# Second attention: the third chunk's transposes inside the next slab, and one output taken ahead of the third exponentials

## The chip, the cores and the metric

One core of one Trainium2 chip runs the kernel in one launch. The metric is device time in microseconds (us), the median of several runs; lower is better. TensorE (PE in the profile) multiplies and transposes, VectorE (DVE) and ScalarE (ACT) do the elementwise work and read PSUM, SyncE (SP) queues the weight loads, GpSimd (POOL) queues three loads and does nothing else.

## The reference

Two transformer-like blocks over 512 tokens of width 1024, in fp32. The change touches the second block's attention alone, a banded attention with 16 query heads, 4 key and value heads, blocks of 128 queries and a band of three key blocks:

```python
scores = jnp.einsum("bnqkgd,bnskd->bnkgqs", qb, kb)
scores = jnp.where(valid[None, :, None, None], scores + alibi, NEG_INF_2)
m = jnp.maximum(jnp.max(scores, axis=-1, keepdims=True), sink_l)
p = jnp.exp(scores - m)
denom = jnp.sum(p, axis=-1, keepdims=True) + jnp.exp(sink_l - m)
o = jnp.einsum("bnkgqs,bnskd->bnqkgd", p / denom, vb)
```

Beside it the same block computes `u` and `g_lru`, two projections of the normalised input; `u` goes through a depthwise convolution over four tokens, `g_lru` through a gelu.

## The kernel before, in words

**Slabs.** All weights stream through the chip as slabs of 512 KB (`load`, line 390). ScalarE rounds each slab to a high part (`split`, line 427), VectorE subtracts to get the low part (`split`, line 823), and TensorE multiplies in three terms: high by high, high by low, low by high. `gemm` (line 1411) does one slab: in the second attention 8 tiles of three matmuls each, 24 matmuls of 128x512, into one PSUM bank. Its argument `then` maps a tile's number to something that TensorE does right after that tile. A slab waits for its low part, and for the bank to be read out.

**Units.** The second attention (`Attention` object `att2`) has 16 units: 4 query blocks, and for each 4 groups of four heads. The first and the last query block have two key chunks in their band, the middle ones three, so units 0 to 3 and 12 to 15 have two chunks and units 4 to 11 three. For one unit the chain is: TensorE computes scores (line 1571), VectorE makes logits (line 1066), their maximum (line 1073) and three tiny operations (1074 to 1077), ScalarE takes exponentials (lines 580 and 583), TensorE transposes them chunk by chunk (line 1602, four transposes for a chunk), ScalarE copies each transposed chunk to SBUF (line 607), TensorE spreads the inverse sums (line 1582) and multiplies by the values (line 1612), ScalarE copies that out (`take_outputs`, line 589) and VectorE scales it (`outputs`, line 1088).

**Slabs between units.** Each unit is paired with one slab of other work, so that TensorE has something to do: slab 0 stands after scores 0, and slab u + 1 between unit u's transposes and its product with the values. Even slabs give `u`, odd slabs the gelu input. The `u2` and `g2` slabs all go to one PSUM bank (`PLACE`, bank 0 of `gp`), so slab k + 1 can't start until ScalarE has read slab k out. For an even slab that is one copy (`inputs2` on ScalarE, line 697, by way of `take`, line 486, its ACTIVATE on line 489), after which VectorE runs the convolution (lines 1299 to 1304). For an odd slab ScalarE first rounds the convolution's result (line 704) and then takes the gelu (also line 489), which needs another function table than the exponentials do. VectorE takes the low part of the convolution's result (`a_low`, line 855).

**The order of each engine** is written out by hand and each engine works strictly through it.

- ScalarE, for each u (`attention`, line 569): take outputs of u - 1; copy the transposed chunks of u; split a slab; exponentials of u + 2; `gate(u + 1)`, which reads out slab u + 1.
- VectorE, for each u (`attention`, line 1052): inverse sums of u + 1; outputs of u - 1; logits of u + 2; then `between(u + 1)`: split a slab, then the convolution or the low part.
- TensorE, for each u (`attention`, line 1562): transposes of chunks 0 and 1; scores of u + 2; the transposes of chunk 2, where there is one; slab u + 1; inverse sums spread; product with the values.

**Waits that matter here.** The transposed chunks alternate between two banks, so a chunk's transposes wait for ScalarE's copy of the chunk two before it (`pt_ready`): chunk 2 waits for the copy of chunk 0. The exponentials alternate between two buffers (`A.logit[u % 2]`), so VectorE's logits of u + 2 overwrite what unit u's transposes read, and wait until all of them are done:

```python
                    if u >= 2:
                        dve.wait_ge(pt_done, A.done[u - 2])
```

The first attention (`att1`) uses the same code with two chunks at most.

Of the kernel before, what the change touches and what calls it, by code (L numbers as in the profile page):

```python
# [68 lines left out]
STAGE = [("zb", 0)]  # L69
# [3 lines left out]
SLAB, _n = {}, 0  # L73
# [24 lines left out]
MIX_SLAB = {key: SLAB["mix"] + i for i, key in enumerate(STAGE)}  # L98
MIX_GATES = [key for key in STAGE if key[0] != "lru"]
# [22 lines left out]
def build(nc, slabs, params, s5p, s5bt, s5b, s5c, bias1, nd2, x_in, out):  # L122

    ctx = ExitStack()
    with ctx:
# [3 lines left out]
        def sem(name):  # L129
            return ctx.enter_context(nc.semaphore(name))  # L130
# [129 lines left out]
        nb_ready, ex_done = sem("maximum_ready"), sem("exponentials_done")  # L260
# [95 lines left out]
        att1 = Attention(0, 0, 1, 1, 0, Q, KV, 0, 1, VT1, logit1, PT1, "sinks", "y1")  # L356
        att2 = Attention(len(att1.units), att1.done[-1], 2, 1, 1, Q2, KV2, 0, 2, VT2, logit2, PT2, "sinks2", "")

        def by_heads(v):
            return v.rearrange("p (h q) -> p h q", h=2)  # L360
# [63 lines left out]
        def _(act):  # L424
            S = Tally(act, act_step)

            def split(n):

                if n >= NSLAB:
                    return  # L430
                act.wait_ge(s_raw[n % RAW], 16 * (n // RAW + 1))
                if n >= RING:
                    act.wait_ge(half_done, 2 * (n - RING + 1))
                nc.scalar.activation(w_hi[:, n % RING, :], raw[:, n % RAW, :], ACT.Copy).then_inc(w_hi_ready, 1)  # L434
# [110 lines left out]
            n = 0  # L545
# [23 lines left out]
            def attention(A, slab0, gate):  # L569

                for pp in range(A.pairs):
                    act.wait_ge(vt_done, pp + 1 + (A.u0 > 0))
                    nc.scalar.activation(A.vt[:, pp, :, :].rearrange("p a b -> p (a b)"), mp[:, 3 + pp, :],
                                         ACT.Copy).then_inc(vt_ready, 1)

                def exponentials(u):
                    row = mini[u % 3]
                    lo, hi = A.span(u)
                    act.wait_ge(nb_ready, A.u0 + u + 1)
                    nc.scalar.activation(row[:, 3, :], row[:, 2, :], ACT.Exp)  # L580
                    for h in range(4):
                        L = A.logit[u % 2][:, h, lo:hi]
                        ins = nc.scalar.activation(L, L, ACT.Exp, bias=row[:, 1, h:h + 1], scale=1.0 / A.units_of_logit,  # L583
                                                   accum_out=row[:, 4, h:h + 1])
                    ins.then_inc(ex_done, 1)

                def take_outputs(u):
                    act.wait_ge(at_done, A.u0 + u + 1)
                    nc.scalar.activation(A.of_heads(A.q, u), by_heads(mp[:, 5, 0:2 * P]), ACT.Copy).then_inc(at_copied, 1)

                def outputs_hi(u):
                    act.wait_ge(at_read, A.u0 + u + 1)
                    nc.scalar.activation(A.of_heads(h_hi, u), A.of_heads(A.q, u), ACT.Copy).then_inc(h_hi_ready, 1)

                n = len(A.units)
                split(slab0 + AHEAD)
                exponentials(0)
                gate(0)
                exponentials(1)
                if A.name:  # L600
                    z_chunk(CT - 1)
                for u in range(n):
                    if u:
                        take_outputs(u - 1)
                    for g, j, _ in A.chunks[u]:
                        act.wait_ge(pt_done, g + 1)
                        nc.scalar.activation(A.pt[:, j, :], mp[:, 3 + g % 2, :], ACT.Copy).then_inc(pt_ready, 1)
                    if A.name and u:
                        outputs_hi(u - 1)
                    if u + 1 < n:  # L610
                        split(slab0 + u + 1 + AHEAD)
                    if u + 2 < n:
                        exponentials(u + 2)
                    if u + 1 < n:
                        gate(u + 1)
                take_outputs(n - 1)
                if A.name:
                    outputs_hi(n - 1)

            def gate_s(u):  # L620
                take("gate_s", u, gate2[u], func=ACT.Tanh, scale=0.5)

            attention(att1, SLAB["gate_s"], gate_s)


# [784 lines left out]
        def _(pe):  # L1410
# [52 lines left out]
            def a_stage(name, k, ready=None, then={}):  # L1463
                gemm(name, k, 8, 1, a, al, ready, then=then)
# [97 lines left out]
            def attention(A, between):  # L1562
                def scores(u):
                    b, pp, _ = A.units[u]
                    lo, hi = A.span(u)
                    k_lo, k_hi = A.keys(u)
                    for i, p, h4, _ in A.lanes(u):
                        rows = slice(HD * p, HD * p + HD)
                        if A.u0 + u:
                            pe.wait_ge(lane_read, 4 * (A.u0 + u - 1) + i + 1)  # L1570
                        pe.matmul(A.scores(i)[:, lo:hi], A.q[rows, 4 * pp + h4, b * P:(b + 1) * P],  # L1571
                                  A.kt[rows, A.k0 + pp, k_lo:k_hi], start=True, stop=True).then_inc(sc_done, 1)

                def spread_inverse(u):

                    pe.wait_ge(inv_ready, A.u0 + u + 1)
                    if A.u0 + u:
                        pe.wait_ge(at_read, A.u0 + u)
                    for h in range(2):
                        for p in range(2):  # L1580
                            lane = mini[u % 3][:, 5, 2 * p + h:2 * p + h + 1]
                            pe.matmul(mp[HD * p:HD * p + HD, 5, (2 + h) * P:(3 + h) * P], lane.to_broadcast([P, HD]), ident,
                                      start=True, stop=True, skip_group_check=True)

                n = len(A.units)
                scores(0)
                between(0)
                scores(1)
                if A.name:
                    outputs(CT - 1)  # L1590
                    pe.wait_ge(z_val, CT)
                pe.wait_ge(vt_ready, A.pairs + (A.u0 > 0))
                for u in range(n):
                    b, pp, _ = A.units[u]
                    pe.wait_ge(ex_done, A.u0 + u + 1)
                    for x, (g, j, kb) in enumerate(A.chunks[u]):
                        if x == 2 and u + 2 < n:
                            scores(u + 2)
                        if g >= 2:
                            pe.wait_ge(pt_ready, g - 1)  # L1600
                        for h in range(4):
                            ins = pe.transpose(mp[:, 3 + g % 2, h * P:(h + 1) * P],  # L1602
                                               A.logit[u % 2][:, h, j * P:(j + 1) * P], ident)
                        ins.then_inc(pt_done, 1)
                    if u + 2 < n and len(A.chunks[u]) < 3:
                        scores(u + 2)
                    between(u + 1)
                    spread_inverse(u)
                    for x, (g, j, kb) in enumerate(A.chunks[u]):
                        pe.wait_ge(pt_ready, g + 1)  # L1610
                        for p in range(2):
                            ins = pe.matmul(mp[HD * p:HD * p + HD, 5, 0:2 * P], A.vt[:, pp, kb, HD * p:HD * p + HD],  # L1612
                                            A.pt[:, j, 2 * P * p:2 * P * (p + 1)], start=x == 0,
                                            stop=x == len(A.chunks[u]) - 1, skip_group_check=True)
                    ins.then_inc(at_done, 1)
# [16 lines left out]
            pe.wait_ge(v_read, CT)  # L1632
            pe.wait_ge(out_read, OUT["gate_a"] + 7)
            transpose_values(att1)
            attention(att1, lambda u: a_stage("gate_s", u) if u < len(att1.units) else None)
            pe.wait_ge(h_lo_ready, H_AT["y1"] + len(att1.units))
            for j in range(COUNT["branch_a"]):
                gemm("branch_a", j, 4, 2, h, hl)
# [32 lines left out]
                    a_stage(name, k)  # L1671
            pe.wait_ge(out_read, OUT["v2"] + 2)
            transpose_values(att2)
            def mix_slab(key):
                gemm("mix", MIX_SLAB[key] - SLAB["mix"], 8, 1, h, hl, first=MIX_GATES.index(key))

            def inputs2(u):
                if u == 0:
                    pe.wait_ge(h_lo_ready, H_AT["xn"] + DC)
                if u < len(att2.units):  # L1680
                    gemm("u2", u, 8, 1, h, hl)
                else:
                    pe.wait_ge(lane_read, 4 * (att2.u0 + len(att2.units)))
                    mix_slab(STAGE[0])

            attention(att2, inputs2)

# [194 lines left out]
```

## Time and profile before

| | |
|---|---|
| Median of 3 runs | 1509.76 us (1509.2 to 1511.92) |
| The profiled execution's own time | 1511.41 us |
| Its span in the profile | 1509.6 us |
| TensorE busy | 1432.3 us, 95% |
| VectorE busy | 867.6 us, 57% |
| ScalarE busy | 619.9 us, 41% |
| The second attention | about 786 to 959 us of the span |
| Granted TensorE clock over the span, mean | 0.981 |

The time is a little more than the span, since it includes what lies around the recorded instructions. Times inside the profile count from the span's start. A busy share says how much of the span an engine worked, not whether anybody waited for it: for that the chain of waits and the timelines have to be read.

### The profile page before, as it was taken

What the parts mean: (1) busy time and instruction counts of PE and PEld (TensorE: products, weight loads), DVE (VectorE), ACT (ScalarE), POOL (GpSimd) and SP (SyncE); (2) the same over time, 40 slices, a digit from 0 to 9 for tenths busy, and PEclk for the clock granted to TensorE, in tenths of its full rate; (3) what the DMA queues carried; (4) which work ended last, traced back from release to release, by engine and by line L of the source; (5) the groups of instructions that cost most, each with busy time, mean ns of one, the idle gap of its engine ahead of it and who ended that gap; (6) DMA issues with size and microseconds to landing.
All of it is one profiled execution on the core that took longest, in us unless ns stands there. A gap on an engine that the chain in (4) does not pass through costs nothing.

```text
span 1509.6 us, 17696 instructions
## 1 busy us (share of the span) xinstructions
PE 1432.3 (95%) x7240; PEld 1153.6 (76%) x7240; DVE 867.6 (57%) x1227; ACT 619.9 (41%) x986; POOL 1.9 (0%) x7
## 2 busy tenths in 40 slices
PE   6999999998999999998998999989799999999997
PEld 5877677777788888887776667767588888888885
DVE  7887644646636364455567766488754443443445
ACT  5452653333313222233245677778543221232232
POOL 0000000000000000000000000000000000000000
PEclk9999999999999999998999999999999999999998
DMA  4222123231323323233131111222232232333323
GB/s 160 88 81 89 54 70 126 86 110 34 112 88 95 111 84 111 85 98 98 44 97 56 43 56 57 77 69 78 84 98 73 96 109 87 98 98 99 97 88 108
DMA packets 36560, 131.62 MB, mean 87 GB/s; under 512 B 4432, under 2 KB 4560, under 8 KB 36224
## 3 DMA queue, kind: packets, MB, share of 16 engines
q1 hardware_dynamic: 36128, 127.16, 26.9%
q0 software_dynamic: 352, 3.34, 0.6%
q8 instruction: 57, 0.93, 0.3%
q14 instruction: 23, 0.19, 0.0%
HBM read 128.39 MB, written 2.10 MB: 86 GB/s over the span
## 4 chain that ended last, share of the span: by engine, by line
PE 74%; DVE 15%; ACT 8%; issue 2%; DMA 1%; SPq 0%; DVEq 0%; ACTq 0%
PE gp L1426 21%; PE gp L1427 21%; PE gp L1428 21%; DVE w_lo L828 2%; ACT arena L583 2%; DVE arena L1066 1%; DVE arena L1073 1%; ACT w_hi L434 1%; PE mp L1602 1%; ACT a_hi L458 1%; PE mp L1571 1%; PE mp L1452 1%; PE mp L1612 1%; PE mp L1426 1%; PE mp L1427 1%
## 5 line engine op out<-in xcount | busy, mean ns | idle before, releaser
L1426 PE MATMUL gp<-h_hi,w_hi 128*128 128x512 f32 x944 | 374.5, 397 | 24.9 <-ACT arena L719 13.5
L1427 PE MATMUL gp<-h_lo,w_hi 128*128 128x512 f32 x944 | 371.0, 393 | 0.0
L1428 PE MATMUL gp<-h_hi,w_lo 128*128 128x512 f32 x944 | 370.7, 393 | 0.0
L828 DVE TENSOR_TENSOR w_lo<-raw,w_hi 128x1024 fp32r<-128x1024 f32 x232 | 283.2, 1222 | 147.9 <-ACT w_hi L434 146.9
L434 ACT ACTIVATE w_hi<-raw 128x1024 fp32r<-128x1024 f32 x232 | 243.1, 1051 | 165.8 <-DMA raw<-slabs 92.9
L1426 PE MATMUL gp<-a_hi,w_hi 128*128 128x512 f32 x704 | 276.3, 393 | 1.2 <-DVE w_lo L828 1.1
L1428 PE MATMUL gp<-a_hi,w_lo 128*128 128x512 f32 x704 | 274.1, 389 | 0.0
L1427 PE MATMUL gp<-a_lo,w_hi 128*128 128x512 f32 x704 | 274.0, 389 | 0.0
L1426 PEld LDWEIGHTS gp<-h_hi,w_hi 128*128 128x128 f32 x944 | 179.5, 190 | 68.8 <-issue 24.7
L1428 PEld LDWEIGHTS gp<-h_hi,w_lo 128*128 128x128 f32 x944 | 179.4, 190 | 38.2
L1427 PEld LDWEIGHTS gp<-h_lo,w_hi 128*128 128x128 f32 x944 | 179.8, 190 | 36.5
L1426 PEld LDWEIGHTS gp<-a_hi,w_hi 128*128 128x128 f32 x704 | 132.1, 188 | 32.3 <-issue 3.3
L1428 PEld LDWEIGHTS gp<-a_hi,w_lo 128*128 128x128 f32 x704 | 132.2, 188 | 27.9
L1427 PEld LDWEIGHTS gp<-a_lo,w_hi 128*128 128x128 f32 x704 | 132.2, 188 | 26.6
L668 ACT ACTIVATE h_hi<-arena 128x512 fp32r<-128x512 f32 x32 | 20.2, 632 | 133.4 <-DVE arena L1205 133.4
L1388 DVE TENSOR_TENSOR arena<-gp,R 128x512 f32<-128x512 f32 x44 | 30.4, 692 | 69.0 <-PE gp L1428 68.9
L804 ACT ACTIVATE a_hi<-arena 128x512 fp32r<-128x512 f32 x22 | 13.9, 633 | 99.5 <-DVE arena L1391 99.5
L1230 DVE TENSOR_TENSOR arena<-arena,gp 128x512 f32<-128x512 f32 x24 | 16.5, 687 | 64.5 <-PE gp L1428 64.5
L489 ACT ACTIVATE arena<-gp 128x512 f32<-128x512 f32 x41 | 24.4, 596 | 63.7 <-PE gp L1428 62.4
L583 ACT ACTIVATE arena<-arena 128x256 f32<-128x256 f32 (+2 forms) x96 | 49.8, 520 | 0.0
L1397 DVE TENSOR_TENSOR arena<-arena,gp 128x512 f32<-128x512 f32 x24 | 16.5, 686 | 57.9 <-PE gp L1428 57.9
L801 ACT ACTIVATE arena<-arena 128x512 f32<-128x512 f32 x22 | 13.9, 632 | 83.5 <-DVE arena L1388 83.5
(248 smaller groups left out, 1505.5 us busy)
## 6 DMA issues: line engine op xcount, KB each, us to landing
raw<-slabs SPq DMA_DIRECT2D x232, 512.0 KB, 3.5
arena<-x_in SPq DMA_DIRECT2D x4, 512.0 KB, 5.8
arena<-x_in POOLq DMA_DIRECT2D x1, 2048.0 KB, 8.7
out_t<-arena SPq DMA_DIRECT2D x8, 256.0 KB, 2.2
arena<-bias POOLq DMA_DIRECT2D x1, 1024.0 KB, 5.2
arena<-s5b SPq DMA_DIRECT2D x1, 512.0 KB, 9.2
arena<-s5c SPq DMA_DIRECT2D x1, 512.0 KB, 10.0
par<-params SPq DMA_DIRECT2D x1, 232.0 KB, 2.6
```

The source lines that it names most:

```text
L434: nc.scalar.activation(w_hi[:, n % RING, :], raw[:, n % RAW, :], ACT.Copy).then_inc(w_hi_ready, 1)
L458: nc.scalar.activation(a_hi[:, c, :], X[:, c, :], ACT.Copy, scale=col(gain, c)).then_inc(a_hi_ready, 1)
L489: nc.scalar.activation(dst, bank(name, m) if src is None else src, func, scale=scale).then_inc(out_read, 1)
L583: ins = nc.scalar.activation(L, L, ACT.Exp, bias=row[:, 1, h:h + 1], scale=1.0 / A.units_of_logit, accum_out=row[:, 4, h:h + 1])
L668: nc.scalar.activation(h_hi[:, k, :], fbuf[k % 2], ACT.Copy).then_inc(h_hi_ready, 1)
L828: TT(w_lo[:, n % RING, :], raw[:, n % RAW, :], w_hi[:, n % RING, :].bitcast(F32), ALU.subtract).then_inc(w_lo_ready, 1)
L1230: TT(Fo[:, m, :], Fo[:, m, :], src, ALU.add).then_inc(out_read, 1)
L1388: TT(tmp[e], take("ff2", s0 + 2 * c + e), R[:, :], ALU.mult).then_inc(out_read, 1)
L1397: TT(X[:, m, :], X[:, m, :], src, ALU.add).then_inc(out_read, 1)
L1426: pe.matmul(dst, hi, x_hi(t), start=t == 0, stop=False)
L1427: pe.matmul(dst, hi, x_lo(t), start=False, stop=False)
L1428: ins = pe.matmul(dst, lo, x_hi(t), start=False, stop=t == tiles - 1)
```

## The change

Two edits, both in the second attention alone. (1) On TensorE the transposes of a unit's third chunk are no longer issued ahead of slab u + 1 but inside it, right behind its tile number 2, that is after nine of its 24 matmuls; scores of u + 2 stand directly in front of the slab, as for units with two chunks. (2) On ScalarE, in the first iteration (u = 0), `gate(1)`, which rounds the first convolution's result and takes the gelu of slab 1, stands ahead of the third exponentials (those of unit 2), not behind them. For all other u the order is as it was. Nothing is added to or taken from what is computed or loaded.

```diff
@@ ScalarE, attention
                     if u + 1 < n:
                         split(slab0 + u + 1 + AHEAD)
+                    if u == 0 and not A.name:
+                        gate(1)
                     if u + 2 < n:
                         exponentials(u + 2)
-                    if u + 1 < n:
+                    if u + 1 < n and (u or A.name):
                         gate(u + 1)
@@ TensorE, attention
                     b, pp, _ = A.units[u]
-                    pe.wait_ge(ex_done, A.u0 + u + 1)
-                    for x, (g, j, kb) in enumerate(A.chunks[u]):
-                        if x == 2 and u + 2 < n:
-                            scores(u + 2)
+                    def turn_chunk(g, j, u=u):
                         if g >= 2:
                             pe.wait_ge(pt_ready, g - 1)
                         for h in range(4):
                             ins = pe.transpose(mp[:, 3 + g % 2, h * P:(h + 1) * P],
                                                A.logit[u % 2][:, h, j * P:(j + 1) * P], ident)
                         ins.then_inc(pt_done, 1)
-                    if u + 2 < n and len(A.chunks[u]) < 3:
+
+                    pe.wait_ge(ex_done, A.u0 + u + 1)
+                    for g, j, _ in A.chunks[u][:2]:
+                        turn_chunk(g, j)
+                    if u + 2 < n:
                         scores(u + 2)
-                    between(u + 1)
+                    third = A.chunks[u][2:]
+                    between(u + 1, {2: lambda: turn_chunk(*third[0][:2])} if third else {})
                     spread_inverse(u)
@@ TensorE, inputs2 and mix_slab
-                    gemm("u2", u, 8, 1, h, hl)
+                    gemm("u2", u, 8, 1, h, hl, then=then)
                 else:
                     pe.wait_ge(lane_read, 4 * (att2.u0 + len(att2.units)))
-                    mix_slab(STAGE[0])
+                    mix_slab(STAGE[0], then)
```

`between` for the first attention takes the new argument and leaves it unused.

## Rows read from the trace of the kernel before

**Rows 1.** Stretches: length, busy of PE, PEld, DVE, ACT, POOL, granted clock, DMA.

```profile
808.00:830.00 22.00, 20.69 (x106) 15.28 (x108) 14.19 (x31) 13.76 (x32) 0.00 (x0) 0.85 0.17 57
...
852.00:874.00 22.00, 21.00 (x128) 15.14 (x128) 15.29 (x29) 15.31 (x35) 0.00 (x0) 1.00 0.15 49
```

**Rows 2.** Who waited for whom, 786 to 960 us: total, times, longest.

```profile
DVE arena L1066 <- PE mp L1602: 3.1, 4, 0.8
PE mp L1602 <- ACT arena L607: 3.0, 3, 1.4
```

**Rows 3.** Chain that ended last, 842 to 865 us: start us, us, what.

```profile
842.69 1.87 DVE arena L1066 x4
...
849.56 0.52 ACT a_hi L704
...
851.40 0.60 ACT arena L489
...
864.48 1.87 DVE arena L1066 x4
```

**Rows 4.** TensorE's timeline: start us, us, line, operation, count, idle before and its releaser.

```profile
804.91 0.38 PE L1571 MATMUL gp<-arena 64*128 64x256 f32 x1
809.31 0.77 PE L1426 MATMUL gp<-h_hi,w_hi 128*128 128x512 f32 x1 [4.03 <-ACT arena L489]
...
814.14 0.63 PE L1428 MATMUL gp<-h_hi,w_lo 128*128 128x512 f32 x1
...
821.50 0.50 PE L1426 MATMUL gp<-h_hi,w_hi 128*128 128x512 f32 x1
...
823.68 0.39 PE L1426 MATMUL gp<-h_hi,w_hi 128*128 128x512 f32 x1
...
831.22 0.47 PE L1426 MATMUL gp<-h_hi,w_hi 128*128 128x512 f32 x1
```

**Rows 5.** ScalarE's timeline, 804 to 818 us, same columns.

```profile
804.57 0.20 ACT L580 ACTIVATE arena<-arena 128x4 f32<-128x4 f32 x1 [3.59 <-DVE arena L1077]
...
807.28 1.28 ACT L489 ACT_TABLE_LOAD   x1
808.57 0.60 ACT L489 ACTIVATE arena<-gp 128x512 f32<-128x512 f32 x1
...
813.11 0.21 ACT L580 ACTIVATE arena<-arena 128x4 f32<-128x4 f32 x1 [0.45 <-DVE arena L1077]
...
817.65 0.60 ACT L489 ACTIVATE arena<-gp 128x512 f32<-128x512 f32 x1 [2.36 <-PE gp L1428]
```

**Rows 6.** VectorE's timeline, 800 to 822 us, same columns.

```profile
800.32 0.75 DVE L1304 SCALAR_TENSOR_TENSOR arena<-arena,par 128x511 f32<-128x511 f32 x1
...
818.28 0.55 DVE L1299 TENSOR_SCALAR arena<-arena,par 128x512 f32<-128x512 f32 x1 [4.07 <-ACT arena L489]
...
821.69 1.48 DVE L1066 SCALAR_TENSOR_TENSOR arena<-arena,mp 128x384 f32<-128x384 f32 x3
```

**Rows 7.** TensorE's timeline round a third chunk's transposes, 840 to 853 us.

```profile
840.84 0.66 PE L1602 MATMUL mp<-par,arena 128*128 128x128 f32 x4
...
850.88 0.48 PE L1571 MATMUL gp<-arena 64*128 64x384 f32 x1
852.81 0.66 PE L1602 MATMUL mp<-par,arena 128*128 128x128 f32 x4 [1.44 <-ACT arena L607]
```

**Rows 8.** Timelines of ScalarE (the gelu of slab 13) and TensorE (slab 14's start).

```profile
934.23 0.60 ACT L489 ACTIVATE arena<-gp 128x512 f32<-128x512 f32 x1
...
935.95 0.50 PE L1426 MATMUL gp<-h_hi,w_hi 128*128 128x512 f32 x1
```

**Rows 9.** TensorE's timeline after two waits elsewhere.

```profile
396.01 0.47 PE L1426 MATMUL gp<-h_hi,w_hi 128*128 128x512 f32 x1 [2.40 <-issue]
...
1037.23 0.77 PE L1426 MATMUL gp<-h_hi,w_hi 128*128 128x512 f32 x1 [2.83 <-ACT arena L719]
...
1039.93 0.47 PE L1426 MATMUL gp<-h_hi,w_hi 128*128 128x512 f32 x1
```

More of the change, by code:

```diff
@@ L1634, in _ @@
             transpose_values(att1)
-            attention(att1, lambda u: a_stage("gate_s", u) if u < len(att1.units) else None)
+            attention(att1, lambda u, then={}: a_stage("gate_s", u) if u < len(att1.units) else None)
             pe.wait_ge(h_lo_ready, H_AT["y1"] + len(att1.units))
@@ L1673, in _, with mix_slab, inputs2 @@
             transpose_values(att2)
-            def mix_slab(key):
-                gemm("mix", MIX_SLAB[key] - SLAB["mix"], 8, 1, h, hl, first=MIX_GATES.index(key))
-            def inputs2(u):
+            def mix_slab(key, then={}):
+                gemm("mix", MIX_SLAB[key] - SLAB["mix"], 8, 1, h, hl, first=MIX_GATES.index(key), then=then)
+            def inputs2(u, then={}):
                 if u == 0:
```

## The prediction

> **What bounds the kernel now.** I read the page's busy shares first (TensorE 95%), then the busy time by stretch: in the second attention TensorE is busy 20.69 to 21.00 of 22 us, VectorE and ScalarE some 14 to 15, and the clock is below full in one stretch alone [rows 1]. That looks like a stage bound by TensorE. The waits say otherwise: TensorE's third-chunk transposes stood for ScalarE's copy three times, 3.0 us in all, and VectorE's logits stood for those transposes four times, 3.1 us in all [rows 2]. So VectorE and ScalarE wait in a ring, and the chain of waits runs through them, not through TensorE.
>
> The ring in the part with three chunks, from the chain: logits of unit 6 start at 842.69, ScalarE reaches the rounding for the gelu at 849.56 and the gelu at 851.40, done 852.00; TensorE's third-chunk transposes follow at 852.81 and are done at 853.47; logits of 7 come right behind, and logits of 8 start at 864.48 [rows 3, 7]. One turn is two units and takes 864.48 - 842.69 = 21.79 us. What TensorE needs for one such unit without waiting is read between the third-chunk transposes of unit 4 (840.84) and the end of the next scores (850.88 + 0.48 = 851.36): 10.52 us, so 21.04 for two [rows 7]. TensorE has 0.75 us to spare in each turn. Nobody waits for it but VectorE, at the third-chunk transposes.
>
> Earlier there is one large hole: scores of unit 3 end at 804.91 + 0.38 = 805.29, and slab 2 starts at 809.31, after 4.03 us, since its bank is freed by the gelu of slab 1. Behind the hole the clock is at the lower level (1.2 GHz): matmuls come every 0.43 us until about 814.6, where 13 have gone by; at the upper level (2.4 GHz) nine take 823.68 - 821.50 = 2.18 us, with the start of a slab in it [rows 4, 5].
>
> **Edit 2, the gelu ahead of the third exponentials.** The gelu of slab 1 needs the first convolution (done at 800.32 + 0.75 = 801.07 [rows 6]) and slab 1, which ends some 0.6 us later. ScalarE is free at 801.0. New order: rounding 0.52 [rows 3], one table load (1.29 from start to next start [rows 5]), gelu at about 803.0, done 803.6 (0.60 [rows 5]). TensorE comes to slab 2 at 805.29, so the 4.03 us are gone, and with them the slow stretch: 13 matmuls of 0.43 against about 0.24, 2.5 us. On TensorE alone that is 6.5 us.
>
> The ring gets less. The exponentials' table goes in from 803.5 to 804.8, so those of unit 2 start at 804.84 in place of 804.57 [rows 5] and end at 807.0. Inverse sums and outputs on VectorE take it to 807.7. Logits of a unit with two chunks take 3.3 us to the exponentials (3.50 from the convolution's end at 801.07 to 804.57, with 0.2 of inverse sums in it [rows 5, 6]). So exponentials of unit 3 start at 810.9 or 811.0, not at 813.11, and need no table load: the loads are as many as before, two, and both now stand ahead of unit 2. They end at 813.1. Slab 2 (24 matmuls, 5.8 us) ended at 811.1, so its copy comes at 813.1, not 817.65, and is done at 813.7; the convolution starts then, not at 818.28 [rows 5, 6]. Everything up to the logits of unit 4 (821.69 before) moves with it: **4.6 us gained**. It is kept as long as the ring is the bound.
>
> A rule of the Trainium skill speaks against this edit: "ScalarE: Activation LUTs", section What ACT_TABLE_LOAD costs, gives every switch of table set some 1.28 us of load and 1.38 us of drain behind it. The trace agrees with the load (1.28 [rows 5]) and not with a drain: the gelu starts 1.29 us after its load did. By the page's figures both switches ahead of unit 2's exponentials would cost 2.8 us more, the gain would be 1.8, and the sum below 2.8 us higher.
>
> **Edit 1, the transposes inside the slab.** Their four waits don't go away: the buffer that VectorE's logits overwrite is still free only when the third chunk is turned. Before, in units 5, 7, 9 and 11, they came 0.81 us behind the gelu (852.00 to 852.81). Now the slab comes first. It can't start before the gelu frees the bank, at 852.00 in the same count; then nine matmuls take 2.18 us, and the change from slab to transposes about 0.1 (my estimate, from 0.32 against 0.23 at a slab's start). The transposes start 2.28 us behind the gelu, the logits 1.47 us later than before. Four times: **5.9 us lost**, all on the ring.
>
> Unit 4 is the first with three chunks. Its transposes were early enough before (840.84 + 0.66 = 841.50, logits at 842.69). Now slab 4 starts behind the gelu of slab 3, 4.6 us earlier than 831.22 at 826.6; slab 5 follows after 840.84 - 831.22 = 9.62 at 836.2; the transposes are done at 836.2 + 2.28 + 0.66 = 839.2, while VectorE is ready at 842.69 - 4.6 = 838.1. **1.1 us lost**. In units 6, 8 and 10 the convolution (3 us on VectorE) covers them, by 0.2 us only: slab 6 at 848.5, slab 7 at 859.2, transposes done 862.1, VectorE ready 862.4. If that cover fails, some tenths each are added.
>
> **At the end** part of the delay is absorbed. Slab 14 started at 935.95 when TensorE got there, 1.12 us after the gelu of slab 13 was done (934.23 + 0.60 = 934.83); from there on TensorE is never waiting long [rows 8]. A ring that is later by 5.9 + 1.1 - 4.6 = 2.4 us moves slab 14 by 2.4 - 1.1 = **1.3 us**. What stands behind the second attention starts from its end and moves with it. Taking TensorE out of a slab and back costs it about 0.2 us in eight units, 1.6 us, hidden in its waits. VectorE's and ScalarE's splits are covered: ScalarE's behind the third copy has still over a microsecond before the exponentials. SyncE's loads follow VectorE's splits, and are two slabs ahead. The first attention has two chunks at most: nothing.
>
> **The clock.** TensorE now needs 21.2 us of a turn of 21.79 + 1.47 = 23.3, and the 2 us between come in one piece, ahead of slabs 6, 8 and 10 (and 1.9 ahead of slab 4: it gets there at 815.0 + 9.7 = 824.7, the gelu at 826.6). A wait of 1.44 us kept the clock [rows 7], so did one of 2.40 behind slab matmuls [rows 9]; one of 2.83 and one of 4.03 lost it [rows 4, 9]. The new ones lie between, and stand behind transposes and scores. Prices: the short slow stretch, six matmuls in 2.70 us against 1.45, costs 1.25 [rows 9]; at most nine slow matmuls stand ahead of the transposes, 9 x 0.2 = 1.8. I take one loss at 1.5; the bounds are none and four of 1.8.
>
> **Sum.** 1.3 + 1.5 = +2.8 us. It is made against the profiled execution (span 1509.6, own time 1511.41, so 1.8 around it). That execution lies 1.65 above the median of 1509.76; I add the difference to the median: 1512.5.
>
> **Rivals.**
> - *The clock falls at three or four of the new waits.* For: they recur with each turn, behind narrow work. Against: 2.40 held. Price 1.3 + 3.5 x 1.5 to 1.3 + 4 x 1.8, so +6.5 to +8.5: 1516.3 to 1518.3. It decides from the second loss on: two give +4.3, beyond 3.0 us, which is 0.2% and about what a measurement of this kernel can tell from no change. Slower. Two or more: 0.33.
> - *TensorE is the bound after all.* For: 95% busy. Then the change gives the hole and slow stretch (6.5), and the 3.0 us of waits ahead of slabs [rows 2], less 1.6 for the broken slabs: -7.9, 1501.9. Against: the ring's 21.79 against 21.04. Weaker form: VectorE's wait costs less than worked, and part of the 4.6 is kept, -3 to 0. Together 0.17.
> - *Table switches cost more in the new place*: +5.6, 1515.4. Against: the row. 0.03.
> - *It doesn't do what it says*: if slab 1 or the convolution came late, ScalarE would stand at the gelu with the exponentials behind it. Both are there within 1 us of need; 0.03, about +1 to +3.
>
> **Numbers.** Forecast (none or one loss of the clock, errors of some tenths in the terms) 0.44, own range 1510.3 to 1514.0. For 8 in 10 the range reaches up to four losses at 1.6 (+7.7) and down to half of the 4.6 us kept (-2.3): 1507.5 to 1517.5. Slower by over 0.2%: 0.33 and 0.03 from the rivals of the clock and the tables, 0.05 from the upper end of the forecast's own range, 0.41. Faster by over 0.2%: 0.11 of TensorE's 0.17. Within: the rest, 0.48.
>
> **What would show it.** Right: slab 2 starts near 805.3 with no wait; the convolution of slab 2 near 813.7; in the chain a turn of about 23.2 in place of 21.8; VectorE's waits for line 1602 at 2.2 us, not 0.8; TensorE's waits ahead of slabs 4, 6, 8, 10 for line 489, 1.7 to 2 us each, and none for line 607; the mix stage about 1 to 3 us later. Wrong: logits of 7, 9, 11 directly behind VectorE's own work, or a turn of 21.8 or less; then the price of edit 1 falls away. Slow matmuls (0.43 apart) behind several of the new waits would be the first rival.

## The result, and the profile after

Over 22 runs of each on one chip the kernel after takes 1514.28 us (1511.63 to 1517.67), the kernel before 1511.97 (1509.01 to 1514.63). The ratio of the times is 1.0018, with an interval of 1.0011 to 1.0024: the change costs about 2.7 us (0.0018 x 1511.97). The interval excludes that nothing changed, and the value lies just under the 0.2% that I called no change. 22 runs put before 2.2 us above the 1509.76 of its first three, so differences are read below, not absolute times. The profiled execution after has a span of 1512.3 us and an own time of 1514.08, against 1509.6 and 1511.41 before.

The busy time of the kernel after by stretch in the second attention (columns: stretch, its length, then busy time with number of instructions of TensorE, its weight loads, VectorE, ScalarE and GpSimd; last the clock, the DMA share and GB/s):

```profile
808.00:830.00 22.00, 19.85 (x116) 14.24 (x115) 16.67 (x34) 14.57 (x33) 0.00 (x0) 1.00 0.18 58
852.00:874.00 22.00, 19.95 (x121) 14.15 (x120) 14.79 (x29) 14.44 (x33) 0.00 (x0) 0.99 0.16 49
```

Against [rows 1], the first stretch is at full clock now (0.85 before), and TensorE is busy a microsecond less in the second: it waits more. Where, the waits say (786 to 962 us; who waited for whom, total us, times, longest):

```profile
ACT arena L607 <- PE mp L1601: 17.4, 10, 3.3
...
DVE arena L1068 <- PE mp L1601: 10.9, 6, 3.2
PE gp L1428 <- ACT arena L489: 9.9, 7, 2.1
```

VectorE's logits (line 1068, 1066 before) stood 3.1 us for the transposes [rows 2] and stand 10.9 now. (The edits move line numbers: the transposes, 1602 before, are 1601 after, 1599 in experiment 2 and 1604 in experiment 9; a slab's matmuls, 1426 to 1428 before, are 1428 to 1430.) The longest of these waits is ahead of the logits of unit 9, behind the transposes of unit 7:

```profile
875.70 1.48 DVE L1068 SCALAR_TENSOR_TENSOR arena<-arena,mp 128x384 f32<-128x384 f32 x3 [3.20 <-PE mp L1601]
```

TensorE's waits for ScalarE's third copy are gone from the list, and its waits ahead of slabs for the gelu (line 489) are 9.9 us. The chain of waits, 800 to 880 us:

```profile
803.12 0.60 ACT arena L489
...
813.31 0.49 ACT arena L489
813.83 0.56 DVE arena L1301
...
817.32 1.87 DVE arena L1068 x4
...
839.20 1.96 DVE arena L1068 x4
...
847.99 0.61 ACT arena L489
848.74 0.47 PE gp L1428
...
851.03 0.45 PE mp L1601 x4
851.50 1.96 DVE arena L1068 x4
...
862.47 1.87 DVE arena L1068 x4
```

The gelu of slab 1 is done at 803.72, the convolution of slab 2 starts at 813.83, the logits of unit 4 at 817.32 (818.28 and 821.69 before [rows 6]): 4.4 us gained. Then the slab and the transposes stand in the chain between the gelu and the logits of unit 7, and the turn from unit 6 to unit 8 takes 862.47 - 839.20 = 23.27 us, not the 21.79 of [rows 3]. TensorE's timeline (start, length, engine, line, operation; in brackets the idle time before it and who ended it):

```profile
805.28 0.50 PE L1428 MATMUL gp<-h_hi,w_hi 128*128 128x512 f32 x1
...
826.77 0.47 PE L1428 MATMUL gp<-h_hi,w_hi 128*128 128x512 f32 x1 [2.15 <-ACT arena L489]
...
848.74 0.47 PE L1428 MATMUL gp<-h_hi,w_hi 128*128 128x512 f32 x1 [1.72 <-ACT arena L489]
850.87 0.60 PE L1601 MATMUL mp<-par,arena 128*128 128x128 f32 x4
...
871.92 0.47 PE L1428 MATMUL gp<-h_hi,w_hi 128*128 128x512 f32 x1 [2.05 <-ACT arena L489]
...
874.18 0.63 PE L1430 MATMUL gp<-h_hi,w_lo 128*128 128x512 f32 x1
874.61 1.05 PE L1601 MATMUL mp<-par,arena 128*128 128x128 f32 x4
876.31 0.63 PE L1430 MATMUL gp<-h_hi,w_lo 128*128 128x512 f32 x1
...
938.30 0.47 PE L1428 MATMUL gp<-h_hi,w_hi 128*128 128x512 f32 x1 [0.87 <-ACT arena L489]
```

Slab 2 starts without a wait. The waits ahead of slabs 4, 6 and 8 are 2.15, 1.72 and 2.05 us, slab 10's is 1.73. In the second attention the lower clock (0.63 us a matmul in place of 0.39 to 0.40) comes once, in slab 8. There the transposes start 874.61 - 871.92 = 2.69 us behind the slab's start (2.13 in slab 6) and take some 0.45 longer: 1.0 us. That is the 3.20 in place of the 2.2 us of VectorE's other waits at odd units. The turn that holds it, by VectorE's timeline from 862.39 to 886.85, takes 24.46 us, 1.27 more than the 23.19 of the turn before it. Slab 14 starts 2.35 us later than in [rows 8].

ScalarE's timeline shows the two table loads, the second right behind the gelu:

```profile
801.82 1.28 ACT L489 ACT_TABLE_LOAD   x1
803.12 0.60 ACT L489 ACTIVATE arena<-gp 128x512 f32<-128x512 f32 x1
803.73 1.28 ACT L580 ACT_TABLE_LOAD   x1
805.03 0.20 ACT L580 ACTIVATE arena<-arena 128x4 f32<-128x4 f32 x1
```

Gelu and exponentials start 1.30 us after their loads began.

### The profile page after: what moved, and what is told of

It reads as the page before. It is cut to its first block, busy times and chain, and to the rows that moved or that the text cites. A ratio compares the mean times of both kernels' runs of the same rounds, so it can differ in the third digit from the quotient of the medians.

```text
span 1512.3 us, 17696 instructions
## 1 busy us (share of the span) xinstructions
PE 1433.1 (95%) x7240; PEld 1153.9 (76%) x7240; DVE 867.4 (57%) x1227; ACT 618.5 (41%) x986; POOL 1.9 (0%) x7
## 4 chain that ended last, share of the span: by engine, by line
PE 72%; DVE 15%; ACT 9%; issue 2%; DMA 1%; SPq 0%; DVEq 0%; ACTq 0%
PE gp L1428 21%; PE gp L1429 20%; PE gp L1430 20%; DVE w_lo L830 2%; ACT arena L583 2%; ACT w_hi L434 1%; DVE arena L1068 1%; DVE arena L1075 1%; PE mp L1601 1%; PE mp L1573 1%; DMA raw<-slabs 1%; ACT a_hi L458 1%; PE mp L1454 1%; PE mp L1616 1%; PE mp L1428 1%
```

## The experiments

My theory: edit 2 (the gelu first) gives 4.6 us, edit 1 (the transposes inside the slab) costs more than that, since VectorE and ScalarE, not TensorE, set the turn. The rivals: TensorE is the bound; or it is the break of the slab itself that costs. Each kernel was timed against the kernel before on the same chip; the table stands at the end of this section. A useful measure within one profile is the length of the stage, from the first transposes of values to the first matmul behind the attention: 175.00 us before (785.09 to 960.09), 177.27 after (785.15 to 962.42). It is of use because the start of the stage lies anywhere from 785.09 to 787.30 us in the twelve profiles, behind work that no edit touches, so whole profiled executions differ by up to 2.2 us that have nothing to do with the change.

**1. Edit 2 alone.** Only the change in ScalarE's order; the transposes stay in front.

> Edit 2 alone: ScalarE takes slab 1's gelu ahead of the third exponentials, the third chunk's transposes stay in front of the slab. Theory R (the ring of VectorE and ScalarE sets the pace): 4.5 us faster than the kernel before (3.5 to 5.5), slab 2 near 805.3, logits of unit 4 near 817.3, a turn of 21.7 to 21.8 us as before. Rival T (TensorE sets the pace): 6.5 us faster, the 4.0 us hole and the 2.5 us of slow matmuls. A table switch with a drain behind it would leave 1.8.

Measured: ratio 0.997, interval 0.996 to 0.9981, so -4.5 us; the stage is 171.04 us, 3.96 shorter, with one loss of the clock in it. The prediction's 4.6 holds, the gain isn't eaten by tables, and it isn't the 6.5 us that TensorE as the bound would have gained.

**2. Edit 1 alone.** Only the change in TensorE's order; the gelu stays behind.

> Edit 1 alone: the third chunk's transposes inside the slab behind tile 2, ScalarE's order as before. R: 5.7 us slower without any loss of the clock, 6 to 8.5 with what the new waits of TensorE (1.7 to 2.0 us ahead of slabs 6, 8, 10) cost in clock; a turn of 23.2 us. T: 1.4 us faster (3.0 us of waits gone, 1.6 for the broken slabs). Rival B (the cost of edit 1 is TensorE's way out of a slab and back, eight times some 0.7 us, wherever in the slab it stands): 5.7 slower too; the next two runs tell B from R.

Measured: 1.0045, 1.0032 to 1.0058, +6.8 us; stage +7.45. Its waits, same stage:

```profile
PE gp L1426 <- ACT arena L489: 12.2, 7, 4.0
DVE arena L1066 <- PE mp L1599: 11.3, 5, 3.8
```

The same waits as after, with the 4 us hole ahead of slab 2 still among them. The two edits alone make -4.5 + 6.8 = +2.3, together +2.7: they add up. With TensorE as the bound it would have been 1.4 us faster by the expectation above.

**3 and 4. Another place inside the slab.** Both edits, the transposes behind tile 0 (three matmuls) or tile 4 (fifteen) instead of tile 2 (nine).

```diff
-                    between(u + 1, {2: lambda: turn_chunk(*third[0][:2])} if third else {})
+                    between(u + 1, {0: lambda: turn_chunk(*third[0][:2])} if third else {})
```

> Both edits, but the transposes behind tile 0 of the slab, three matmuls in, not nine. R: they are then ready about when ScalarE's copy is, as before the change; 4.7 us faster than the kernel before (3.5 to 5.5), 7 us faster than the changed one, a turn of 21.8, TensorE's waits ahead of slabs 6, 8, 10 at 0.7 us and no slow matmuls behind them. T: 7.9 faster. B: 2.7 slower, like the changed kernel.

> Both edits, the transposes behind tile 4, fifteen matmuls in. R: each of the four odd units costs 1.37 us more and the convolution no longer covers the even ones (another 0.8 each): 10.4 us slower than the kernel before without clock losses, 12 to 15 with them, since TensorE's waits grow to 3.05 us; a turn of 25.3. B: 2.7 slower, as behind tile 2. T: nothing, or faster.

Measured: behind tile 0 0.9975, 0.9964 to 0.9987, -3.8 us; behind tile 4 1.0112, 1.0095 to 1.0128, +16.9. TensorE's timeline behind tile 0:

```profile
848.06 0.47 PE L1428 MATMUL gp<-h_hi,w_hi 128*128 128x512 f32 x1 [0.69 <-ACT arena L489]
848.84 0.60 PE L1601 MATMUL mp<-par,arena 128*128 128x128 f32 x4
```

The transposes start 0.78 us behind the slab here. Behind the gelu's end (847.93) they start 0.91 us later, and before it was 0.81 [rows 3, 7]. The time is that of edit 2 alone but for 0.7 us, the intervals overlap, and the turn is 21.85 us. So the break of a slab costs next to nothing: what costs is the matmuls ahead of the transposes. Behind tile 4 the slab runs 883.64 - 880.10 = 3.54 us first. The chain of waits of that kernel:

```profile
842.39 1.96 DVE arena L1068 x4
...
858.85 1.96 DVE arena L1068 x4
870.56 1.96 DVE arena L1068 x4
...
896.00 1.96 DVE arena L1068 x4
...
923.04 1.42 DVE arena L1068 x4
```

The turn from 870.56 to 896.00 takes 25.44 us at full clock, for an expected 25.3. The turns on either side hold a loss of the clock and take 28.17 and 27.04, so the two losses cost 2.7 and 1.6. The profile has a third loss, in slab 14, behind a wait of 2.08 us: eight matmuls come 0.43 us apart and not 0.23, with TensorE never waiting from there to the end of the stage, which is another 1.6. The expected 10.4 without losses and these 5.9 make 16.3, and the profiled stage is 16.39 longer. So the expected 12 to 15 was too low by the number and the price of the losses. TensorE's timeline has three waits of 3.09 us; the first matmul behind each:

```profile
851.93 0.77 PE L1428 MATMUL gp<-h_hi,w_hi 128*128 128x512 f32 x1 [3.09 <-ACT arena L489]
...
880.10 0.47 PE L1428 MATMUL gp<-h_hi,w_hi 128*128 128x512 f32 x1 [3.09 <-ACT arena L489]
...
905.54 0.64 PE L1428 MATMUL gp<-h_hi,w_hi 128*128 128x512 f32 x1 [3.09 <-ACT arena L489]
```

The same wait at the same place of the loop lost the clock twice and kept it once.

**5 and 6. Inside the slab for half the units.** The prediction has all of the price in the odd units (5, 7, 9, 11) and holds the even ones (6, 8, 10) covered. So the third chunk of odd units (experiment 5) or of even units (experiment 6) was put back in front:

```diff
                     third = A.chunks[u][2:]
+                    if third and u % 2 == 1:
+                        turn_chunk(*third[0][:2])
+                        third = []
```

(experiment 6 has `== 0`.)

> Both edits, but only units 4, 6, 8 and 10 turn their third chunk inside the slab (behind tile 2); units 5, 7, 9 and 11 turn it in front of the slab, as before. By the prediction's account the convolution covers the even units but for unit 4: 3.5 us faster than the kernel before. Worked through once more with the odd units' transposes in front, TensorE reaches the even units' slabs later, the 0.2 us of cover are not there, VectorE waits 1.7 us at each, and it is 1.2 us slower than before, a turn of 23.4. This run tells whether that cover belongs to the even units or to the delay of the odd ones.

> Both edits, but only units 5, 7, 9 and 11 turn their third chunk inside the slab; the even ones in front of it. The odd units' 1.47 us each stay, the 1.1 us of unit 4 go: 0.2 us slower than the kernel before without clock losses, up to 2 slower with them; a turn of 23.2. If the break of a slab were the cost, this and the run with the even units would each give half of what both cost.

Measured: even units inside the slab 1.0031, 1.0022 to 1.0041, +4.7 us; odd units inside 1.0, 0.9991 to 1.0008, no difference. The prediction's account, by which the first would have been 3.5 us faster, is wrong; the second working in the expectation (1.2 slower, a turn of 23.4) has the sign and the turn. The chain of waits with even units inside:

```profile
866.09 1.96 DVE arena L1068 x4
...
889.57 1.96 DVE arena L1068 x4
```

The turn is 23.48 us, about as long as with all units inside. With odd units inside it is 23.22, from the chain of waits of experiment 6:

```profile
839.82 1.87 DVE arena L1068 x4
...
863.04 1.87 DVE arena L1068 x4
```

What is saved against after is the delay of unit 4 (the logits of unit 6 start 839.82 - 786.77 = 53.05 us behind the start of the stage, 54.05 in after) and, in the profiles, the loss of the clock, which experiment 6 doesn't have. So the delays of odd and even units don't add: a turn of 21.79 grows to about 23.3 if either half is delayed. The convolution covers an even unit only while VectorE comes to it late, and it came late because of the odd unit's delay. Taking that away makes VectorE ready 1.47 us earlier and the transposes no earlier; the cover of 0.2 becomes a wait of about 1.3 by this sum, and of 1.61 in the profile, at full clock:

```profile
889.57 1.48 DVE L1068 SCALAR_TENSOR_TENSOR arena<-arena,mp 128x384 f32<-128x384 f32 x3 [1.61 <-PE mp L1601]
```

Besides, TensorE now stood for the third copy ahead of odd transposes for longer:

```profile
851.37 1.11 PE L1601 MATMUL mp<-par,arena 128*128 128x128 f32 x4 [2.40 <-ACT arena L607]
852.13 0.78 PE L1428 MATMUL gp<-h_hi,w_hi 128*128 128x512 f32 x1
```

and the clock was lost there, though not behind two more waits of 2.40 us at the same place of the loop. With the corrected cover the sum is +1.2 us, and one loss of the clock makes it +2.2 to +2.7; the profiled stage is 2.59 longer. The span of this profile is 4.9 us longer than that of before (1514.5 against 1509.6), but 2.05 of it stand ahead of the stage, which starts at 787.14 and not at 785.09. So the account holds for the stage as profiled. Why the medians differ by 4.7 (interval 3.3 to 6.2), some 2 more than the stage, isn't settled; more losses of the clock in the other executions would do it, and no run shows them.

**7 and 8. The gelu first for every second slab.** If VectorE and ScalarE set the turn because the gelu stands behind the exponentials, the remedy is edit 2 for all odd slabs. The number of table loads stays the same.

```diff
-                    if u == 0 and not A.name:
-                        gate(1)
+                    if u % 2 == 0 and not A.name:
+                        gate(u + 1)
...
-                    if u + 1 < n and (u or A.name):
+                    if u + 1 < n and (u % 2 or A.name):
```

Experiment 8 has the transposes behind tile 0 as well.

> The changed kernel with edit 2 carried to every odd slab (1, 3, 5, ... 15): ScalarE takes its gelu ahead of the exponentials of the unit behind it; the transposes inside the slab behind tile 2. If the odd units' cost of edit 1 is the gelu that stands between the exponentials and the slab, it goes: TensorE no longer waits for line 489 ahead of slabs 4 to 14, a turn is 21.5 us, and it is 8.5 us faster than the kernel before. If the price is the nine matmuls as such, a turn stays at 23.2 and only the later start of some units is saved: 1 to 2 us faster than the changed kernel.

> As the run before, with the transposes behind tile 0. A turn of 20.5 us on VectorE and ScalarE is then below what TensorE needs (21.0 to 21.2), TensorE becomes the bound: 8.7 us faster than the kernel before, hardly more than behind tile 2. The candidate for the best version.

Measured: 0.9942, 0.993 to 0.9955, -8.8 us, and 0.9949, 0.9936 to 0.9961, -7.7. Both beat both kernels, and aren't told apart. The waits of experiment 7, same stage:

```profile
ACT arena L580 <- DVE arena L1079: 20.6, 9, 3.3
...
DVE arena L1068 <- PE mp L1601: 7.7, 5, 1.9
ACT arena L489 <- PE gp L1430: 6.4, 4, 2.2
...
PE gp L1428 <- ACT arena L489: 0.2, 1, 0.2
```

TensorE's 9.9 us of waits for the gelu have become 0.2, and ScalarE's gelu waits for TensorE instead. TensorE's timeline:

```profile
844.90 0.50 PE L1428 MATMUL gp<-h_hi,w_hi 128*128 128x512 f32 x1
...
847.08 0.60 PE L1601 MATMUL mp<-par,arena 128*128 128x128 f32 x4
...
855.46 0.50 PE L1428 MATMUL gp<-h_hi,w_hi 128*128 128x512 f32 x1
```

From slab to slab TensorE takes 10.56 us, so 21.12 a turn, and from the start of the stage to its end it has no wait over 0.25 us: now it is the bound. VectorE still waits 7.7 us for transposes, and that costs nothing any more.

**9. The gelu first, the transposes in front.** Before, with ScalarE's order of experiment 7: edit 1 undone in the best version.

> The gelu first for every odd slab, as in the run e7, but the third chunk's transposes in front of the slab: edit 1 undone. If edit 1 is harmful only because the slab waits for the gelu, then its sign turns once the gelu is out of the way: in front of the slab TensorE stands for ScalarE's copy at the odd units, inside it doesn't, so this run is 2 us slower than the ones with the transposes inside, 6.3 us faster than the kernel before. If the transposes inside the slab cost in any order, this run is the fastest of all, 10 us or more faster.

Measured: 0.9967, 0.9955 to 0.9979, -5.0 us; stage 168.92 us against 165.81 in experiment 7. Its waits:

```profile
PE mp L1604 <- ACT arena L607: 3.8, 4, 1.0
...
DVE arena L1068 <- PE mp L1604: 3.1, 4, 0.8
```

TensorE stands for the third copy before every second third chunk, 3.8 us in all. So edit 1, which costs 6.8 us by itself, is worth some 3 to 4 us here (3.8 by the two ratios, 3.1 by the stages): its sign depends on the order of the gelu.

**10. The gelu first for slabs 1 and 3 only.** After, with `u in (0, 2)` as the condition, the first step from after towards experiment 7.

> The changed kernel with the gelu first for slabs 1 and 3 alone. TensorE's wait ahead of slab 4 (2.15 us in the changed kernel's profile) goes, with any loss of the clock behind it; the turns behind it stay at 23.2 us. 0.7 us faster than the kernel before, 2 us faster than the changed one; more than 3 us better than the changed one would mean that the clock was often lost at slab 4.

Measured: 1.0006, 0.9998 to 1.0015, +0.9 us, 1.8 below after where 2 was expected, and by its interval not to be told from before: only the first turns are freed, and the later ones keep their price.

The times, medians in us; the last column is the difference of the profiled stage to that of before (175.00), which is one execution each.

| kernel | this | before | ratio, interval | us by the ratio | stage |
|---|---|---|---|---|---|
| after | 1514.28 | 1511.97 | 1.0018, 1.0011-1.0024 | +2.7 | +2.27 |
| 1 edit 2 alone | 1507.56 | 1512.11 | 0.997, 0.996-0.9981 | -4.5 | -3.96 |
| 2 edit 1 alone | 1519.31 | 1512.11 | 1.0045, 1.0032-1.0058 | +6.8 | +7.45 |
| 3 behind tile 0 | 1508.16 | 1512.11 | 0.9975, 0.9964-0.9987 | -3.8 | -4.94 |
| 4 behind tile 4 | 1529.73 | 1512.11 | 1.0112, 1.0095-1.0128 | +16.9 | +16.39 |
| 5 even units | 1516.9 | 1512.76 | 1.0031, 1.0022-1.0041 | +4.7 | +2.59 |
| 6 odd units | 1512.71 | 1512.76 | 1.0, 0.9991-1.0008 | 0 | 0.00 |
| 7 gelu first | 1503.17 | 1512.76 | 0.9942, 0.993-0.9955 | -8.8 | -9.19 |
| 8 and tile 0 | 1504.7 | 1512.76 | 0.9949, 0.9936-0.9961 | -7.7 | -8.57 |
| 9 and in front | 1506.1 | 1512.04 | 0.9967, 0.9955-0.9979 | -5.0 | -6.08 |
| 10 slabs 1 and 3 | 1513.04 | 1512.04 | 1.0006, 0.9998-1.0015 | +0.9 | +0.43 |

## Why the prediction was right, point by point

- **What bounds the kernel.** Right: VectorE and ScalarE in a ring. Filling TensorE's hole ahead of slab 2 gained 4.5 us where 6.5 would have come had it been the bound (experiment 1), taking away its waits at the third chunk made the kernel slower (2), and only with the gelu out of the ring (7) does TensorE set the turn.
- **Edit 2, 4.6 us gained.** Right: 4.4 in the chain, 4.5 by itself.
- **No drain behind a table load.** The exponentials start 1.30 us after their load began, and the edit's gain is 4.5. By the 1.38 us of drain that the Trainium skill, "ScalarE: Activation LUTs", section What ACT_TABLE_LOAD costs, gives beside the load for every switch of set, 1.8 would have been left, an estimate (4.6 less two drains). The trace agrees with the page on the load (1.28) and not on the drain, and the measurement decides: that rival is gone.
- **Edit 1, 1.47 us in each odd unit, 1.1 in unit 4.** Right in size: turn 23.27 for a worked 23.3, logits of unit 6 at 839.20 for a worked arrival of the transposes at 839.2. VectorE's waits at the odd units are the forecast 2.2 us (2.18, 2.19, 2.20) but for one of 3.20, which holds the 1.0 us of the slow clock in slab 8.
- **The even units are covered.** Right as long as the odd ones are delayed, wrong as a property of the even ones. The step holds only for the change as made. As a general account it failed in experiment 5, which by it would have been 3.5 us faster than before and was 4.7 slower.
- **The end takes up 1.1.** Right: the gelu of slab 13 starts 3.33 us later (937.56, before 934.23) and slab 14 only 2.35, so 0.98 is taken up for a worked 1.1. Of the 2.35, the slow stretch in slab 8 makes 1.0 to 1.27, which leaves 1.1 to 1.35 for a worked 1.3.
- **The break of the slab, 0.2 us in each of eight units.** Too high: about 0.04 (experiment 7). It changes nothing, since the prediction had it hidden in TensorE's waits.
- **The clock, one loss at 1.5.** One loss, of 1.0 to 1.27 us, in the profile; the stage as a whole is 2.27 longer, and 0.4 of the 2.7 us between the two spans stand behind it. One loss was a choice between none and four that the rows did not decide. It came at slab 8 here and in experiments 2 and 10, but whether it comes in most executions isn't shown: no run removed it separately. That the sum of 2.8 meets the 2.7 so closely is luck in this term.
- **The rivals.** The clock falling at three or four waits didn't happen here, but did with longer waits (experiment 4). TensorE as the bound and dearer tables fell. The number, 2.8 us over before, was forecast as it came. The absolute time, 1514.28, lies 1.8 us above the forecast 1512.5 and 0.3 above the forecast's own narrower range (1510.3 to 1514.0), since before itself is 2.2 us above the median that I had added to.

## What to carry to other kernels

Where two engines wait for each other in turn, an engine that is busy 95% need not be the bound: here TensorE became it only when the two were freed. Compare the turn of the chain with what the busiest engine needs for a turn (21.79 against 21.04 us here). If the chain is longer, look for the instruction that stands behind work that doesn't need to be first (here a gelu behind exponentials) and move that, then fill the busy engine's gaps. The order of the steps matters: the move of the transposes costs 6.8 us while the gelu is late, and gains 3 to 4 once it is early. And delays at two places of one turn don't add up, so a cover worked out with one of them in place must not be used without it.

## What was not expected of the hardware

- The length of a wait of 2 to 3 us doesn't decide alone whether TensorE's clock falls to 1.2 GHz. Ahead of slab 4 six profiles have a wait of 2.13 to 2.17 us (after, experiments 1, 3, 4, 5, 6), and the clock fell in one, experiment 1. Ahead of slab 8 three have one of 2.05 or 2.06 (after, experiments 2 and 10), and it fell in all three. Of three waits of 2.40 in experiment 5 it fell behind one, of three of 3.09 in experiment 4 behind two. What else decides is open. A loss cost 1.0 to 2.7 us. In experiment 1 the fall came some 1.2 us after the work had resumed, in the first and third case of experiment 4 right at the first matmul:

```profile
826.97 0.47 PE L1428 MATMUL gp<-h_hi,w_hi 128*128 128x512 f32 x1 [2.16 <-ACT arena L489]
...
828.57 0.63 PE L1428 MATMUL gp<-h_hi,w_hi 128*128 128x512 f32 x1
...
831.13 0.63 PE L1428 MATMUL gp<-h_hi,w_hi 128*128 128x512 f32 x1
```

- Going from a slab to four transposes and back inside an accumulation costs TensorE almost nothing: 10.56 us from slab to slab in experiment 7, where 10.52 had been read for a unit with an unbroken slab (10.47 in experiment 9, from 847.04 to 857.51). I had put 0.2 on each unit.
